# Latent attention in three single-pass products of high and low parts: queries, keys, values and scores

## What is computed

```python
proj = h @ w_in
q_g, k_g, v_g, q_lat, kv_lat = jnp.split(proj, IN_OFFSETS, axis=-1)
...
c_q = rms_norm(q_lat, mla_q_norm)                                   # 256 wide
q_m = (c_q @ w_q_b).reshape(B, S, MLA_HEADS, MLA_QK_DIM)            # 8 heads of 64 + 32
q_m = jnp.concatenate([q_m[..., :MLA_NOPE_DIM], apply_rope(q_m[..., MLA_NOPE_DIM:], cos_m, sin_m)], axis=-1)
c_kv = rms_norm(kv_lat[..., :MLA_KV_RANK], mla_kv_norm)             # 128 wide
k_rope = apply_rope(kv_lat[..., MLA_KV_RANK:].reshape(B, S, 1, MLA_ROPE_DIM), cos_m, sin_m)
kv = (c_kv @ w_kv_b).reshape(B, S, MLA_HEADS, MLA_NOPE_DIM + MLA_V_DIM)
k_m = jnp.concatenate([kv[..., :MLA_NOPE_DIM],
                       jnp.broadcast_to(k_rope, (B, S, MLA_HEADS, MLA_ROPE_DIM))], axis=-1)
v_m = kv[..., MLA_NOPE_DIM:]
o_m = blocked_attention(q_m[:, :, :, None, :], k_m, v_m, MLA_QK_DIM ** -0.5)
```

## Time and profile before

| what | value |
| --- | --- |
| median of three runs | 3004.63 us (3003.12 to 3005.75) |
| profiled execution, span from first to last instruction | 3003.8 us |
| mean granted TensorE clock, as a share of full speed | 0.977 |
| TensorE matmul rows busy | 2816.4 us, 94% |
| VectorE busy | 1422.1 us, 47% |
| ScalarE busy | 1129.1 us, 38% |
| GpSimd busy | 238.4 us, 8% |
| the chain of work that ended last | TensorE 82%, VectorE 7%, loads 4%, ScalarE 4% |
| attention loop of layer 0 | about 79 to 240 us of the span |

### The profile page before, as it was taken

The page is one execution under the profiler, slowest core; times in us unless marked ns, Lnnn a source line. Parts: engine busy times, 40 slices in busy tenths (PEclk is TensorE's granted clock), DMA queues, the critical chain, the costliest instruction groups (busy, mean ns, idle before and its releaser), DMA issues.

```text
span 3003.8 us, 40104 instructions
## 1 busy us (share of the span) xinstructions
PE 2816.4 (94%) x16212; PEld 2094.2 (70%) x16212; DVE 1422.1 (47%) x2150; ACT 1129.1 (38%) x1920; POOL 238.4 (8%) x229
## 2 busy tenths in 40 slices
PE   7999979989999979999999789999999999799998
PEld 5657854536658745447877578888888787578886
DVE  6665532237666333244555763333334654753444
ACT  4664431124665321135233652222222542643332
POOL 0011020000011110001011010000001111000001
PEclk9999989999999989999999899999999999999999
DMA  4011249981002259993435122223320234222220
GB/s 157 29 43 59 86 173 415 415 366 64 29 29 100 100 237 418 414 395 127 144 115 153 40 76 113 112 114 128 124 84 16 88 122 130 81 84 99 98 99 28
DMA packets 67909, 428.28 MB, mean 143 GB/s; under 512 B 7968, under 2 KB 8352, under 8 KB 20368
## 3 DMA queue, kind: packets, MB, share of 16 engines
q1 hardware_dynamic: 62144, 407.96, 35.6%
q0 software_dynamic: 4432, 15.67, 1.6%
q10 hardware_dynamic: 1152, 2.10, 0.2%
HBM read 416.78 MB, written 8.91 MB: 142 GB/s over the span
## 4 chain that ended last, share of the span: by engine, by line
PE 82%; DVE 7%; DMA 4%; ACT 4%; issue 2%; POOL 2%; SPq 0%; DVEq 0%; ACTq 0%; POOLq 0%
PE banks L854 78%; PE banks L855 4%; DMA weight<-in_w_up 3%; ACT arena L1685 3%; DVE arena L2390 3%; POOL arena L3200 2%; DVE arena L3046 1%; DVE arena L2679 0%; DVE weight_part L2494 0%; DMA block_tokens_high<-df_stage 0%; DVE arena L2677 0%; DMA weight<-in_ada_w 0%; ACT weight_part L1685 0%; DVE x L2390 0%; POOL block_tokens_low L3214 0%
## 5 line engine op out<-in xcount | busy, mean ns | idle before, releaser
L1685 ACT ACTIVATE arena<-banks 128x512 f32<-128x512 f32 (+2 forms) x513 | 281.2, 550 | 885.0 <-PE banks L854 779.4
L854 PE MATMUL banks<-weight,arena 128*64 128x512 f32 (+4 forms) x2136 | 429.1, 573 | 21.3 <-DMA weight<-in_w_up 9.2
L854 PE MATMUL banks<-hidden,weight_part 128*128 128x512 f32 (+1 forms) x2304 | 446.8, 355 | 0.0
L854 PEld LDWEIGHTS banks<-hidden,weight_part 128*128 128x128 f32 x2304 | 381.2, 189 | 70.4 <-issue 3.8
L854 PE MATMUL banks<-tokens_high,weight_part 128*128 128x512 f32 (+1 forms) x1536 | 409.0, 357 | 10.0 <-ACT tokens_high L1685 10.0
L2494 DVE TENSOR_TENSOR weight_part<-weight,weight_part 128x2048 fp32r<-128x2048 f32 x124 | 285.8, 2308 | 194.8 <-ACT weight_part L1685 194.7
L1685 ACT ACTIVATE weight_part<-weight 128x2048 fp32r<-128x2048 f32 x124 | 236.4, 1908 | 349.7 <-PE banks L854 336.4
L854 PEld LDWEIGHTS banks<-weight,arena 128*64 128x64 f32 (+2 forms) x2136 | 150.9, 135 | 255.4 <-issue 233.8
L854 PEld LDWEIGHTS banks<-tokens_high,weight_part 128*128 128x128 f32 x1536 | 273.9, 190 | 62.5 <-DVE arena L2390 16.0
L3200 POOL TENSOR_TENSOR arena<-arena 128x512 f32<-128x512 f32 (+1 forms) x89 | 116.0, 1303 | 1974.3 <-ACT arena L1685 1707.4
L854 PE MATMUL banks<-tokens_low,weight_part 128*128 128x512 f32 (+1 forms) x768 | 264.7, 354 | 0.0
(11 more groups left out here) (216 smaller groups left out, 3879.6 us busy)
## 6 DMA issues: line engine op xcount, KB each, us to landing
weight<-in_w_gate SPq DMA_DIRECT2D x64, 1024.0 KB, 13.6
weight<-in_w_up SPq DMA_DIRECT2D x64, 1024.0 KB, 8.1
weight<-in_w_down SPq DMA_DIRECT2D x64, 1024.0 KB, 11.2
weight<-in_w_ff SPq DMA_DIRECT2D x64, 1024.0 KB, 4.8
weight<-in_ada_w SPq DMA_DIRECT2D x48, 1024.0 KB, 6.3
weight<-in_w_in SPq DMA_DIRECT2D x28, 1024.0 KB, 5.2
weight<-in_w_o SPq DMA_DIRECT2D x8, 1024.0 KB, 4.8
weight<-in_w_mem_kv SPq DMA_DIRECT2D x8, 1024.0 KB, 4.9
```

Source lines behind the costliest of these rows:

```text
L854: mm = lambda o, a, b, first=True, last=True: eng.matmul(o, a, b, start=first, stop=last, skip_group_check=True)
L1685: act = lambda o, i, f=ACT.Copy, **k: eng.activation(o, i, f, **k)
```

## The change

The latent attention's products for queries, keys, values and scores go from `tile` to `tile3`. For that:

- `w_kv_b` and `w_q_b` are split too. `w_kv_b` takes the place of the first `w_o` chunk in front of the loop, `w_q_b` is split in step 2, and the three `w_o` chunks in steps 6, 28 and 30 (VectorE 7, 29, 31).
- The latents are split in step 3 (`CQH`, `CQL`, `CKVH`, `CKVL`): three roundings on ScalarE, three subtractions on VectorE.
- Each head's key: ScalarE writes the high part straight from the bank (`KMH`) and, for heads 0 to 5, the rotated rows; VectorE subtracts it from the bank one step later, at the end of `mla_rope`, and this subtraction frees the bank. For heads 0 to 3 a second subtraction makes the low part of the rotated rows. Later heads use the tiles of earlier ones again and find these rows there.
- Each head's query: two steps after its preparation ScalarE rounds it (`mla_high`) and VectorE subtracts (`mla_low`).
- A score waits for `kml` and `qml` of its head.
- The load of the memory tokens moves on GpSimd's queue from head 2 to behind the heads, and waits for the last latent score, since its place in the arena now holds high and low parts.

```diff
@@ -500,7 +500,7 @@
 BLOCK_LOADED, BLOCK_HIGH = (0, 1, 2), (3, 4)
-is_split = lambda key: key[0] in ("w_in", "w_o", "w_mkv", "w_mq", "w_mo", "ff1", "ff2") + IN_BLOCK
+is_split = lambda key: key[0] in ("w_in", "w_kv_b", "w_q_b", "w_o", "w_mkv", "w_mq", "w_mo", "ff1", "ff2") + IN_BLOCK
 IN_BLOCK = ("w_four", "w_u", "w_sv", "w_nq", "w_nk", "w_nv", "w_dv", "w_dq", "w_dk", "w_out")
@@ -607,6 +607,14 @@
 b.update(paired(c, t, T, 4, (2, 2)))
+tiles = lambda name, at, n: Carve(at * T).rounded(f"{name}{l}", n, T)
+b.update(CQL=tiles("latent_q_low", 23, 2), CKVL=tiles("latent_kv_low", 25, 1)[:, 0, :], CQH=tiles("latent_q_high", 39, 2), CKVH=tiles("latent_kv_high", 41, 1)[:, 0, :])
+low = tiles("mla_low", 26, 8)
+first, second, last = tiles("mla_high_a", 8, 4), tiles("mla_high_b", 17, 4), [tiles(f"mla_high_c{at}_", at, 1)[:, 0, :] for at in (16, 21, 22, 42)]
+pairs_of = lambda a: [(a[:, 2 * i, :], a[:, 2 * i + 1, :]) for i in range(2)]
+highs = pairs_of(first) + pairs_of(second) + [tuple(last[0:2]), tuple(last[2:4])] + pairs_of(second)
+b["QMH"], b["KMH"] = [a for a, _ in highs], [k for _, k in highs]
+b["QML"], b["KML"] = [[low[:, 4 * z + h % 4, :] for h in range(HQ)] for z in range(2)]
 b["SQW"] = Ring(st, "SQW" + t, [b["H"][:, k, :] for k in range(KD)])
@@ -838,9 +846,9 @@
-def tile3(key, lhs, rhs, n=T, free=(), needs=()):
-
-    o = PB.take(key)[:, 0:n]
+def tile3(key, lhs, rhs, n=T, free=(), needs=(), rows=P):
+
+    o = PB.take(key)[0:rows, 0:n]
     if PB.former:
@@ -1065,22 +1073,23 @@
         if h == 0:
-            wcur[:] = [weight(("w_q_b", l)), wcur[1]]
+            wcur[:] = [weight_parts(("w_q_b", l)), wcur[1]]
         wq, wkv = wcur
-        eng.wait_ge(*after(("cqn", l)))
-        tile(("qm", l, h), [wq[:, k, P * h:P * h + P] for k in range(2)], [S["CQ"][:, k, :] for k in range(2)],
-             free=(WF(("w_q_b", l)),) if h == HQ - 1 else ())
-        eng.wait_ge(*after(("ckvn", l)))
-        tile(("km", l, h), [wkv[:, P * h:P * h + NOPE]], [S["CKV"]], rows=NOPE,
-             free=(WF(("w_kv_b", l)),) if h == HQ - 1 else ())
+        eng.wait_ge(*after(("cql", l)))
+        tile3(("qm", l, h), halves(wq, h, range(2)), [(S["CQH"][:, k, :], S["CQL"][:, k, :]) for k in range(2)],
+              free=(WF(("w_q_b", l)),) if h == HQ - 1 else ())
+        eng.wait_ge(*after(("ckvl", l)))
+        tile3(("km", l, h), [tuple(a[:, P * h:P * h + NOPE] for a in wkv)], [(S["CKVH"], S["CKVL"])], rows=NOPE,
+              free=(WF(("w_kv_b", l)),) if h == HQ - 1 else ())
...
             h = 2 * j + u[4]
-            eng.wait_ge(*after(("qmr", l, h)))
-            tile(("S", u), [S["QM"].get((l, h))[0:QK, q * P:q * P + P]], [S["KM"].get((l, h))[0:QK, :]],
-                 free=(S["QM"].free((l, h)), S["KM"].free((l, h))) if q == TB - 1 else ())
+            eng.wait_ge(*after(("kml", l, h)))
+            eng.wait_ge(*after(("qml", l, h)))
+            tile3(("S", u), [tuple(a[h][0:QK, q * P:q * P + P] for a in (S["QMH"], S["QML"]))], [tuple(a[h][0:QK, :] for a in (S["KMH"], S["KML"]))],
+                  free=(S["QM"].free((l, h)), S["KM"].free((l, h))) if q == TB - 1 else ())
@@ -1093,10 +1102,11 @@
             if c == 0:
-                eng.wait_ge(*after(("ckvn", l)))
-                wcur.append(weight(("w_kv_b", l)))
+                eng.wait_ge(*after(("ckvl", l)))
+                wcur.append(weight_parts(("w_kv_b", l)))
             wkv = wcur[1]
-            tile(("vm", l, c), [S["CKV"][:, c * P:c * P + P]], [wkv.rearrange("p (h x) -> p h x", x=P)[:, :, NOPE:P]])
+            tile3(("vm", l, c), [tuple(S[n][:, c * P:c * P + P] for n in ("CKVH", "CKVL"))],
+                  [tuple(a.rearrange("p (h x) -> p h x", x=P)[:, :, NOPE:P] for a in wkv)])
         if i in PREP_AT:
@@ -1807,7 +1817,7 @@
     root(("g", l, 4), S)
-    split_high(("w_o", l, 0))
+    split_high(("w_kv_b", l))
     high(3)
@@ -1820,13 +1830,23 @@
         copy(q, ("qm", l, h), PB.get(("qm", l, h)), ("qr", l, h), scale=QK ** -0.5)
-        m = S["KM"].take((l, h))
+        S["KM"].take((l, h))
         if S["KM"].former:
             eng.wait_ge(*after(S["KM"].former))
-        copy(m[0:NOPE, :], ("km", l, h), PB.get(("km", l, h))[0:NOPE, :])
-        eng.wait_ge(*after(("ks", l)))
-        act(m[64:96, :], S["KR"][64:96, :]).then_inc(*done(("kmr", l, h)))
-        eng.wait_ge(scalar_step, done.count)
+        if h == 0:
+            eng.wait_ge(*after(("ks", l)))
+        if h == 2:
+            eng.wait_ge(*after(("out", ("S", ("g", l, 3, TB - 1, 1)))))
+        if h == 4:
+            eng.wait_ge(*after(("out", ("og", l, 3))))
+        eng.wait_ge(*after(("out", ("km", l, h))))
+        act(S["KMH"][h][0:NOPE, :], PB.get(("km", l, h))[0:NOPE, :]).then_inc(*done(("kmh", l, h)))
+        if h < 6:
+            act(S["KMH"][h][64:96, :], S["KR"][64:96, :]).then_inc(*done(("krh", l, h)))
+
+    def mla_high(h):
+        eng.wait_ge(*after(("qmr", l, h)))
+        act(S["QMH"][h][0:QK, :], S["QM"].get((l, h))[0:QK, :]).then_inc(*done(("qmh", l, h)))
@@ -1843,6 +1863,13 @@
             copy(S["KR"][64:128, :], ("kr", l), PB.get(("kr", l))[64:128, :], ("krc", l))
+            split_high(("w_q_b", l))
+        if i == 3:
+            eng.wait_ge(*after(("low", l, 4)))
+            round_tiles([S["CKVH"]], [S["CKV"]], lambda k: ("ckvn", l), lambda k: ("ckvh", l))
+            round_tiles([S["CQH"][:, j, :] for j in range(2)], [S["CQ"][:, j, :] for j in range(2)], lambda j: ("cqn", l), lambda j: ("cqh", l, j))
+        if i - 2 in PREP_AT:
+            mla_high(PREP_AT.index(i - 2))
         if VM_AT <= i < VM_AT + TB:
@@ -1853,8 +1880,8 @@
             round_outputs(0)
-        if i in (6, 10):
-            split_high(("w_o", l, (i - 2) // 4))
+        if i in (6, 28, 30):
+            split_high(("w_o", l, (6, 28, 30).index(i)))
@@ -2496,7 +2523,8 @@
         eng.wait_ge(*after(needs(k)))
-        tt(a, b, h, SUB).then_inc(*done(keys(k)))
+        done_with = keys(k)
+        tt(a, b, h, SUB).then_inc(*done(*(done_with if done_with == () or type(done_with[0]) is tuple else (done_with,))))
@@ -2554,7 +2582,7 @@
     gqa_rope(4)
-    split_low(("w_o", l, 0))
+    split_low(("w_kv_b", l))
     low(3)
@@ -2564,9 +2592,17 @@
         eng.wait_ge(*after(("qc", l, h)))
-        eng.wait_ge(*after(("kmr", l, h)))
         tt(q[R, :], q[R, :], S["TBB"][R, :], ADD).then_inc(*done(("qmr", l, h)))
-        eng.wait_ge(vector_step, done.count)
+        eng.wait_ge(*after(("kmh", l, h)))
+        low, key = S["KML"][h], ("km", l, h)
+        tt(low[0:NOPE, :], PB.get(key)[0:NOPE, :], S["KMH"][h][0:NOPE, :], SUB).then_inc(*done(PB.free(key), *((("kml", l, h),) if h >= 4 else ())))
+        if h < 4:
+            eng.wait_ge(*after(("krh", l, h)))
+            tt(low[R, :], K[R, :], S["KMH"][h][R, :], SUB).then_inc(*done(("kml", l, h)))
+
+    def mla_low(h):
+        eng.wait_ge(*after(("qmh", l, h)))
+        tt(S["QML"][h][0:QK, :], S["QM"].get((l, h))[0:QK, :], S["QMH"][h][0:QK, :], SUB).then_inc(*done(("qml", l, h)))
@@ -2583,6 +2619,11 @@
                   frees=[(PB.free(("ckv", l)),)])
+            split_low(("w_q_b", l))
+        if i == 3:
+            low_tiles([S["CKVL"]], [S["CKV"]], [S["CKVH"]], lambda k: ("ckvh", l), lambda k: ("ckvl", l))
+            low_tiles([S["CQL"][:, j, :] for j in range(2)], [S["CQ"][:, j, :] for j in range(2)], [S["CQH"][:, j, :] for j in range(2)],
+                      lambda j: ("cqh", l, j), lambda j: (("cql", l),) if j else ())
         if i == 4:
@@ -2592,12 +2633,14 @@
             mla_rope(PREP_AT.index(i - 1))
+        if i - 2 in PREP_AT:
+            mla_low(PREP_AT.index(i - 2))
         if i == NG + 8:
...
             out_low(0)
-        if i in (7, 11):
-            split_low(("w_o", l, (i - 3) // 4))
+        if i in (7, 29, 31):
+            split_low(("w_o", l, (7, 29, 31).index(i)))
@@ -3226,12 +3269,10 @@
         eng.wait_ge(pool_step, done.count)
-        if h == 2:
-
-            eng.wait_ge(*after(("out", ("S", ("g", l, 3, TB - 1, 1)))))
-            eng.dma_start(B["mem", l]["MR"], A["mem"].rearrange("(k p) t -> p k t", p=P)).then_inc(small[("mem", l)], 16)
         if h == 4:
             add_squares(S, [(("og", l), T)])
+    eng.wait_ge(*after(("out", ("S", ("m", l, 3, TB - 1, 1)))))
+    eng.dma_start(B["mem", l]["MR"], A["mem"].rearrange("(k p) t -> p k t", p=P)).then_inc(small[("mem", l)], 16)
     add_squares(S, [(("mn", l), CT)])
...
     for other in meet(("mem", l)):
```

## The result

The kernel with the change takes 3056.3 us (3054.1 to 3059.7, median of 4 runs; the kernel before, on the same chip, 3005.2): the ratio is 1.0172, 95% interval 1.0158 to 1.0187. The direction was as forecast, the size was not: +51 us instead of +30, and the time lies above the range (3009 to 3044). The profiled execution has a span of 3057.9 us; the granted clock of the whole span falls from 0.977 to 0.967.

What follows compares the result with a forecast made beforehand. TensorE was taken to bound the kernel. Per layer, 19.2 + 2.0 + 4.7 + 0.3 - 11.1 = 15.1 us longer, 30 us for two, on 3004.6: forecast 3034 us, range 3009 to 3044.

Steps and rivals of the forecast that it cites:

- What bounds the kernel: In the latent heads' stage TensorE bounds: savings come off the span and waits add to it, one for one.
- Savings: TensorE's shorter latent products, scores and values, plus a shorter weight split before the loop: 11.1 us saved a layer.
- the shorter split: Before the attention loop, splitting w_kv_b takes half a w_o chunk's time and ends TensorE's 0.66 us wait for VectorE.
- The key's bank: In the latent heads, TensorE waits for VectorE's later subtraction to free the key's PSUM bank: 19.2 us a layer.
- The last pair's query: At heads 6 and 7, TensorE waits for the query's low part, which no further preparation covers: 2.0 us a layer.
- The start: At the loop's start, the w_q_b split, the latents' split and the key's rotation delay TensorE: 4.7 us a layer.
- Edits at no cost: Moved w_o splits, the later load of mem and ScalarE's query roundings cost nothing, but for about 0.3 us.
- rival D: TensorE's clock falls in the wait of 5 us: 3044 us, or 3050 if GpSimd also holds up low parts; 10%.
- the end: At the end of the loop, where no score follows, moved w_o splits cost about 0.3 us a layer.
- B: Rival: the key's bank is free in time because VectorE runs ahead of TensorE's score; 2998 us, faster; 7%.
- C: Rival: the waits are real but cover each other as VectorE catches up; 3.9 us a layer, 3012 us; 20%.
- E: Rival: the new matmuls take more than one pass; time within that of rival D; 1%.

Runs made afterwards that it cites:

- e3: Kernel after the change, with TensorE repeating a matmul 3 to 19 times before the eight waiting scores, so it stays busy through the waits; 3040.0 us.
- e1: Kernel after the change, with ScalarE copying each key product out of its bank, which frees it at once, and VectorE subtracting from the copy; 3019.1 us.
- e7: Kernel after the change, with VectorE's subtraction on the key's bank moved into the preparing step, behind that step's two maxima; 3015.0 us.
- e4: Kernel before the change, plain float32, with only the key's bank freed by an added VectorE subtraction behind the rotation's add; 3047.9 us.
- e11: e8 with the output norm spread over several steps, one multiply and one low part taken out of step 27, head 1's query split a step earlier; 2997.9 us.
- e2: Kernel after the change, with the subtraction that frees the key's bank moved ahead of the rotation's multiply and add; 3015.9 us.
- e8: e7 with the query weight split in steps 6 and 7 instead of 2, and head 7's query split one step earlier; 3004.5 us.

## Why the prediction was right and wrong

**What bounds the kernel** held: each wait that came or went shows in the time, and so do the savings. But a wait cost more than its length.

**Savings** held. Forecast 11.1 us a layer, 12.1 measured. A full preparation with its score pair takes 165.11 - 161.55 = 3.56 us after, against 4.74; I had 2.24 + 1.56 = 3.80. The 0.2 us for entering the run, which I had charged twice there, is paid once. One term of the savings was wrong: the shorter split didn't end the wait of 0.66 us, which stands in the kernel after as before:

```profile
88.27 0.50 PE L862 MATMUL banks<-gqa_high 64*128 64x512 f32 x2 [0.66 <-DVE arena L2417]
```

The loop starts 0.3 us earlier, and the products and values save 11.8 where I had 10.4. Two of my bounds were also miscounted: with 0.3 us for entering a run the products and values save 7.1 and not 8, and the low end of the forecast's own range to 3019 and not 3022. Neither touches the result.

**The key's bank** held, in place, releaser and length: forecast 2.2, 3.0, 1.25, 1.8, 2.4, 1.1, 5.4, 2.0; measured 2.30, 2.96, 1.18, 1.62, 2.88, 0.98, 4.74, 3.82. One is off. For head 7 I wrote "as head 3", but behind head 6's long wait VectorE first waits 3.69 us for ScalarE's high part of query 6, and then has the norm's low parts (3.59 us at 231.45) in front of the step's reductions. Both follow from the order of work, and I counted neither. Head 4's wait is 0.5 us longer than forecast, since beside GpSimd's sums the multiply takes 1.44 us and not only the add 1.63 (the multiply took 0.90 before). The low parts of the queries, which I had feared for in the same way, were never held up: all sixteen took 0.69 us. The two operations of head 4, and then eight of the sixteen low parts:

```profile
190.81 1.44 DVE L2592 TENSOR_TENSOR arena<-arena 32x512 f32<-32x512 f32 x1
192.28 1.63 DVE L2595 TENSOR_TENSOR arena<-arena 32x512 f32<-32x512 f32 x1
...
L2605 DVE TENSOR_TENSOR mla_low<-arena,mla_high_b 96x512 fp32r<-96x512 f32 x8 | 5.5, 688 | 15.7 <-ACT mla_high_b L1695 15.7
```

**The last pair's query**: 2.0 us forecast, nothing seen. The head's own slow blocks covered it. With the clock kept up it shows as 1.0 (e3), with the bank waits gone as 3.32 (e1) and 2.42 (e7). The mechanism was right, and it was hidden by a bigger one; undoing the bank alone therefore gave less than its length.

**The start** held in its first half: the exponentials start at 102.17 and TensorE waits 2.67 us until 103.09, where I had 3.0 until 103.6. Of the other 1.7 us, for the latents' split and the key's rotation, 0.17 came. That the whole is still near (4.3 against 4.7) is luck: 1.5 of it are work at the lower clock, which was not in the forecast. **Edits at no cost** held: no wait for a `w_o` chunk or for `mem`.

**The step that failed is the clock.** In the sum it stood at nothing. It appears only as rival D, with 10%, and there as "two such waits" of 5 us. The rows that I had were far apart: 1.00 behind a wait of 0.70 us and 0.75 in a stretch in which TensorE was busy 2.0 of 10 us. I put the waits of 1 to 3 us, seven of the eight, on the side of the first row without a reason and left them out of the range too. Measured, the clock fell behind six of the eight waits and behind the start's. The slower work is 14.6 us in layer 0, 13.5 of it the clock's, and as much in layer 1: 27 of the 51 us are the clock. The trace of the kernel before held nearer rows that I had not read. Its busy table for the 2 us behind waits of 5.35, 2.93 and 1.76 us (columns as in the earlier trace rows):

```profile
22.60:24.60 2.00, 2.00 (x5) 1.61 (x6) 2.00 (x4) 1.91 (x4) 0.00 (x0) 0.50 0.87 360
394.24:396.24 2.00, 1.90 (x16) 1.58 (x16) 1.26 (x2) 2.00 (x5) 1.55 (x2) 1.00 0.38 156
1690.57:1692.57 2.00, 2.00 (x8) 1.64 (x8) 1.89 (x5) 0.52 (x2) 0.00 (x0) 0.50 0.00 0
```

They show the lower clock behind a wait as long as the one forecast for head 6, and behind 1.8 and 2.9 us either level. With the 14.6 us in the sum the forecast would have been 15.1 + 14.6 = 29.7 us a layer, and the time 3064 us, above the measured one: without the clock my sum was too high, by the last pair's 2.0, 1.9 of the start and 1.0 of the savings, less 1.3 for the bank and the end. These errors hid part of the miss.

The Trainium skill (TensorE: Matmul & The Clock Gate, "What's actually happening"), which I cited there, says that the throttle is the default and that activity releases it; the traces agree in kind (0.50 behind the wait of 4.74 us, 1.00 in e3 where the same time is filled with matmuls). What it cost had to come from the runs.

**Rivals.** B (the bank is free in time) is out by the eight waits, and e7 shows what it takes: the subtraction ahead of the copy of turned keys and of the rotation. C (the waits cover each other) is out for the bank, and right in the small for the last pair. E is out: three matmuls of 0.23 us each.

**Open.** What decides whether the clock falls behind a wait of middle length wasn't found; layer 0 and layer 1 of one execution differ in it (e4, e11); the counts are below. Nor do the runs say what the 0.24 us is that a wait costs beyond its length at the full clock.

## What to carry to other kernels

When a PSUM bank's release moves from an engine with slack to one with a queue, follow that queue instruction by instruction up to the signal: the order of three VectorE instructions was worth 40 us here (e2), and the same change went from 51 us slower to 6 us faster without one matmul altered. Price a wait of TensorE twice, its length and the work behind it at the lower clock, as soon as it is longer than the waits behind which the trace shows the full clock throughout. And expect the second-latest wait to show up when the latest is gone: e1, e8 and e11 each gained less than what they removed for that reason.

## What the hardware showed that I had not expected

Counted in the attention loops and the norm behind them of all thirteen profiles, both layers (95 to 290 and 750 to 945 us): of 108 waits of TensorE from 0.5 to 1.3 us none was followed by a lower granted clock in the next 4 us; of 58 from 1.3 to 2.6 us 30 were; of 34 longer ones all were. That is a count for this stage and no rule: the wait of 2.93 us at 394.24 in the kernel before was not. The same wait at the same place can go either way: TensorE's 2.0 us wait for GpSimd's sums behind the loop is followed by four matmuls in 1.13 us in the kernel before and in 1.97 us after it, with the same matmuls behind it. The line of the kernel before, and then that of the kernel after:

```profile
257.31 1.13 PE L854 MATMUL banks<-arena,mats 128*128 128x256 f32 x4 [2.02 <-POOL arena L3200]
```

```profile
283.52 1.97 PE L862 MATMUL banks<-arena,mats 128*128 128x256 f32 x4 [2.01 <-POOL arena L3243]
```

Once fallen, the clock cost 1.5 to 3.1 us of work a time in the kernel after, summed over the two steps at the wait and with the 0.2 us that any wait brings, and 3.4 us at most in e4 (layer 1, behind a wait of 2.18 us). Behind the one of 4.74 us the granted clock was still 0.50 in the stretch from 2 to 4 us after it, and step 25 took 2.21 us more than its 6.43.
